# Experts' results that leave by indirect transfers, and norm factors with a token on each partition

## The reference

```python
def rmsnorm_2(x, g):
    xf = x.astype(jnp.float32)
    y = xf * lax.rsqrt(jnp.mean(xf * xf, axis=-1, keepdims=True) + EPS)
    return (y * g.astype(jnp.float32)).astype(x.dtype)

def swiglu_2(t, w_gu, w_dn):
    g, u = jnp.split(t @ w_gu, 2, axis=-1)
    return (jax.nn.silu(g) * u) @ w_dn
```

## Time and profile before

| | |
|---|---|
| three runs | 3429.14, 3432.21, 3434.34 us (median 3432.21) |
| the profiled execution | 3431.26 us, of which the span is 3429.4 |
| mean granted clock of TensorE | 0.983 |
| PE busy | 3291.8 us, 96% |
| DVE, ACT, POOL busy | 2001.3, 1767.8 and 1211.6 us |
| DMA | 555.34 MB; 531.62 read from HBM, 41.94 written |

### The profile page before, as it was taken

One profiled execution on the slowest core, in us unless ns is written; L12 is line 12 of the kernel. 1 busy time (PEld: TensorE's weight loads), 2 busy tenths in 40 slices (PEclk: granted clock), 3 DMA queues, 4 the chain that ended last, 5 costly groups with the idle time before them and its releaser, 6 DMA issues.

```text
span 3429.4 us, 48281 instructions
## 1 busy us (share of the span) xinstructions
PE 3291.8 (96%) x16320; PEld 2646.2 (77%) x16320; DVE 2001.3 (58%) x2489; ACT 1767.8 (52%) x2130; POOL 1211.6 (35%) x625
## 2 busy tenths in 40 slices
PE   8999999999999999999999999898899999999996
PEld 6888887778888788888778888687666788787783
DVE  4335674653353533641663333568766798888887
ACT  5552325455524555321645533324563788888883
POOL 3444441144444344444044444342102222222224
PEclk9999999999999999999999999999899999999998
DMA  3225321022253222533322233222003899999997
GB/s 124 98 98 168 114 95 50 26 88 96 98 169 120 86 98 93 168 118 111 117 92 97 93 96 100 79 92 84 19 14 110 337 401 412 404 408 404 398 400 303
DMA packets 128099, 555.34 MB, mean 162 GB/s; under 512 B 19344, under 2 KB 19600, under 8 KB 100112
## 3 DMA queue, kind: packets, MB, share of 16 engines
q1 hardware_dynamic: 112896, 520.59, 41.6%
q0 software_dynamic: 14976, 33.58, 2.6%
q10 hardware_dynamic: 144, 0.08, 0.0%
HBM read 531.62 MB, written 41.94 MB: 167 GB/s over the span
## 4 chain that ended last, share of the span: by engine, by line
PE 60%; issue 25%; POOL 8%; DVE 5%; ACT 1%; DMA 0%; POOLq 0%; DVEq 0%; ACTq 0%
PE ps L762 17%; PE ps L764 16%; PE ps L763 16%; POOL w_lo L1814 7%; PE ps L1232 2%; PE ps L782 1%; PE ps L922 1%; PE ps L1311 1%; PE ps L947 1%; PE ps L932 1%; PE ps L1043 1%; PE ps L1061 1%; PE ps L1022 1%; PE ps L1251 0%; PE ps L1216 0%
## 5 line engine op out<-in xcount | busy, mean ns | idle before, releaser
L1814 POOL TENSOR_TENSOR w_lo<-stage_buf,w_hi 128x1024 fp32r<-128x1024 f32 (+1 forms) x396 | 971.1, 2453 | 1505.0 <-ACT w_hi L1387 1505.0
L1387 ACT ACTIVATE w_hi<-stage_buf 128x1024 fp32r<-128x1024 f32 (+1 forms) x396 | 413.9, 1045 | 1195.1 <-PE ps L764 1142.4
L762 PE MATMUL ps<-x_hi,w_hi 128*128 128x512 f32 x1984 | 776.4, 391 | 8.9 <-POOL w_lo L1814 7.9
L763 PE MATMUL ps<-x_lo,w_hi 128*128 128x512 f32 x1984 | 775.1, 391 | 0.0
L764 PE MATMUL ps<-x_hi,w_lo 128*128 128x512 f32 x1984 | 774.9, 391 | 0.0
L762 PE MATMUL ps<-hid,w_hi 128*128 128x512 f32 x1312 | 519.0, 396 | 2.6 <-issue 1.7
L764 PE MATMUL ps<-hid,w_lo 128*128 128x512 f32 x1312 | 511.7, 390 | 0.0
L763 PE MATMUL ps<-hid,w_hi 128*128 128x512 f32 x1312 | 510.9, 389 | 0.0
L762 PEld LDWEIGHTS ps<-x_hi,w_hi 128*128 128x128 f32 x1984 | 374.3, 189 | 90.6 <-POOL w_lo L1814 10.2
L764 PEld LDWEIGHTS ps<-x_hi,w_lo 128*128 128x128 f32 x1984 | 374.2, 189 | 78.3
L763 PEld LDWEIGHTS ps<-x_lo,w_hi 128*128 128x128 f32 x1984 | 374.3, 189 | 77.6
(11 more groups left out here) (398 smaller groups left out, 4879.4 us busy)
## 6 DMA issues: line engine op xcount, KB each, us to landing
stage_buf<-in_gu SPq DMA_DIRECT2D x176, 512.0 KB, 3.2
big<-in_exp_gu SPq DMA_DIRECT2D x72, 1024.0 KB, 14.0
h_buf<-in_exp_gu SPq DMA_DIRECT2D x72, 1024.0 KB, 13.9
s_buf<-in_exp_dn SPq DMA_DIRECT2D x72, 1024.0 KB, 13.9
slot_rows<-stage_buf SPq DMA_DIRECT2D x72, 512.0 KB, 13.5
stage_buf<-in_down SPq DMA_DIRECT2D x64, 512.0 KB, 3.6
stage_buf<-in_down SPq DMA_DIRECT2D x32, 384.0 KB, 3.2
sil_buf<-in_ada SPq DMA_DIRECT2D x24, 512.0 KB, 4.1
```

The lines of the kernel that those rows point to most:

```text
L762: nc.tensor.matmul(o, a_hi, b_hi, start=start, stop=False)
L763: nc.tensor.matmul(o, a_hi, b_lo, start=False, stop=False)
L1387: nc.scalar.activation(w_hi[s][:, 0:n], stage[s][:, 0:n], ACT.Copy).then_inc(upper_done, 1)
L1814: nc.gpsimd.tensor_tensor(w_lo[s][:, 0:n], stage[s][:, 0:n], w_hi[s][:, 0:n].bitcast(F32), ALU.subtract).then_inc(parted, 1)
```

## The change

**Results.** SP no longer stores whole blocks. GpSimd writes them with an indirect transfer (`scatter`) that takes each of the 128 rows to its token and choice in `slots`, now [4, 128, 8, 1024]; rows of empty slots are out of bounds and not written. In each turn GpSimd waits for `tx` as before and now also for the evacuation of the block before (`evacuated`), converts two columns of indices, asks for the gather of block n+3, and behind it for the scatter of block n-1. Four scatters follow the loop. The 32 fetches at the end are plain transfers issued by SP. The first turn is written out on ScalarE and GpSimd, as it has nothing to scatter.

**Tables.** The token's number and the choice's go into one value, so `at_b` is made with 32 DVE operations (compare, times the value) in place of four DVE comparisons and four ScalarE scalings; `tab_f` is computed from the result with three more DVE operations; `slot_i` is gone.

**Norm factors.** For four norms (ffn1_0, norm1, first, norm2) and the four heads TensorE's sums go to one column for each 128 tokens (`token_sums`), so root and reciprocal are 128x4. TensorE then spreads the reciprocals over the partitions again (`token_rows`: four matmuls with the unit matrix), and DVE multiplies from PSUM or copies first (`spread_scale`). The table of the root is loaded earlier in two places, and each head's output is made two steps later.

```diff
-        slot_f, slot_i = small[:, 0:32], small[:, 32:64].bitcast(I32)
+        slot_f = small[:, 0:32]
...
-                    def store_rows(i, s):
-                        sp.wait_ge(bk["oev"], i * 2 + (s + 3))
-                        sp.dma_start(dr["slots"][bass.ds(i * 2 + s, 1), :, :].rearrange("a p n -> p (a n)"), o_sb[s].bitcast(I32)
-                                     ).then_inc(o_out[s], 16)
-
...
+                    def fetch(row, t, k, done):
+                        sp.dma_start(row.bitcast(I32), dr["slots"][t, :, k, :]).then_inc(done, 16)
...
+            def token_sums(bank, src, first=True, last=True):
+
+                for t in range(TT):
+                    ins = nc.tensor.matmul(ps[:, bank, t:t + 1], src[:, t * P:t * P + P], ones[:, 0:1],
+                                           start=(first and t == 0), stop=(last and t == TT - 1))
+                return ins
+
+            def token_rows(bank):
+
+                for t in range(TT):
+                    ins = nc.tensor.matmul(ps[:, bank, t * P:t * P + P], inv_tok[:, t:t + 1].to_broadcast([P, P]), eye[:, :],
+                                           start=True, stop=True)
+                return ins
...
-                    def gather(s, b, n):
-
-                        nc.gpsimd.tensor_copy(idx[:, s:s + 1], tab_f[:, b]).then_inc(bk["staged"], 1)
+                    def entry(s, b, n, c0, c1):
+
+                        nc.gpsimd.tensor_copy(idx[:, s, c0:c1], table[:, b, c0:c1]).then_inc(bk["staged"], 1)
                         pool.wait_ge(bk["staged"], n)
                         pool.sem_inc(bk["asked"], 1)
+
+                    def gather(s):
+
                         nc.gpsimd.indirect_dma_start(
                             out=xg[s], out_offset=None, in_=dr["tok"],
-                            in_offset=bass.IndirectOffsetOnAxis(ap=idx[:, s:s + 1], axis=0),
+                            in_offset=bass.IndirectOffsetOnAxis(ap=idx[:, s, 0:1], axis=0),
                             bounds_check=T - 1, oob_is_err=False).then_inc(gathered[s], 16)
 
+                    def evacuated(n):
+                        pool.wait_ge(bk["oev"], n + 2)
+                        pool.sem_inc(bk["asked"], 1)
+
+                    def scatter(s):
+
+                        nc.gpsimd.indirect_dma_start(
+                            out=dr["slots"].rearrange("t p k n -> (t p k) n"),
+                            out_offset=bass.IndirectOffsetOnAxis(ap=idx[:, s, 1:2], axis=0),
+                            in_=o_sb[s].bitcast(I32), in_offset=None,
+                            bounds_check=T * TOP_K - 1, oob_is_err=False).then_inc(o_out[s], 16)
+
...
+                    def one_block(i, s, first=False):
+                        pool.wait_ge(bk["tx"], i * 2 + (s + 2))
+                        pool.sem_inc(bk["asked"], 1)
+                        if not first:
+                            evacuated(i * 2 + s)
+                        entry(1 - s, bass.ds(i * 2 + (s + 3), 1), i * 2 + (s + 4), 0, 1 if first else 2)
+                        gather(1 - s)
+                        if not first:
+                            scatter(1 - s)
+
+                    one_block(0, 0, first=True)
+                    one_block(0, 1)
+                    with pool.Fori(1, more_n) as i:
                         for s in range(2):
-                            pool.wait_ge(bk["tx"], i * 2 + (s + 2))
-                            gather(1 - s, bass.ds(i * 2 + (s + 3), 1), i * 2 + (s + 4))
...
+                            one_block(i, s)
+                    one_block(more_n, 0)
+                    for j in range(4):
+                        evacuated(more_n * 2 + (j + 1))
+                        entry(j % 2, bass.ds(more_n * 2 + (j + 4), 1), more_n * 2 + (j + 5), 1, 2)
+                        scatter(j % 2)
...
             def hgrn_head_out(hd):
 
-                dve.wait_ge(hg["o_std"], hd + 1)
-                link(nc.vector.reciprocal(rstd[:, :], std[:, :]))
+                dve.wait_ge(hg["o_sq"], hd + 1)
                 link(nc.vector.scalar_tensor_tensor(out=mixed[:, hd, :], in0=ps[:, 4 + hd % 2, :],
-                                                    scalar=col("hg_g")[:, hd:hd + 1], in1=rstd[:, :],
+                                                    scalar=col("hg_g")[:, hd:hd + 1], in1=tiles(big[:, R_HG:R_NQ], T)[:, hd, :],
                                                     op0=ALU.mult, op1=ALU.mult))
-                nc.vector.tensor_tensor(mixed[:, hd, :], mixed[:, hd, :], tiles(big[:, R_HG:R_NQ], T)[:, hd, :],
+                dve.wait_ge(factor, FACTOR_AT[f"head{hd}"] + 2)
+                nc.vector.tensor_tensor(mixed[:, hd, :], mixed[:, hd, :], ps[:, 6 if hd < 3 else 7, :],
                                         ALU.mult).then_inc(hg["o_out"], 1)
...
                 dve.wait_ge(tab["filled"], 1)
-                nc.vector.tensor_scalar(tab_f, ps[:, 6, 0:BLOCKS], float(NO_ROW), None, ALU.add).then_inc(tab["in"], 1)
+                link(nc.vector.tensor_scalar(tab_v, ps[:, 6, 0:BLOCKS], float(2 * T * TOP_K), None, ALU.add))
+
+
+                link(nc.vector.tensor_scalar(tab_f, tab_v, 1.0 / TOP_K, 0.5 / TOP_K - 0.5, ALU.mult, ALU.add))
+                link(nc.vector.tensor_scalar(tab_f, tab_f, 12582912.0, None, ALU.add))
+                nc.vector.tensor_scalar(tab_f, tab_f, -12582912.0, None, ALU.add).then_inc(tab["in"], 1)
```

More of the change, by code:

```diff
@@ L249, in block_kernel @@
         SUM_BANK = {n: 3 if n == "first" else 2 if n in ("ffn1_1", "norm1") else 7 for n in NORMS}
+        BY_TOKEN = ("ffn1_0", "norm1", "first", "norm2")
+        FACTOR_AT = {"ffn1_0": 0, "norm1": 2, "first": 4, "head0": 7, "head1": 9, "head2": 11, "head3": 13, "norm2": 15}
+        std_tok, inv_tok = std[:, 8:8 + TT], std[:, 16:16 + TT]
         TILE_N = {n: KD * k for k, n in enumerate(TILEWISE)}
@@ L866, in token_major @@
                         last.then_inc(units_done, 1)
+                        if phase == "tok_2" and c == 0 and n == 0:
+                            spread_factor("first")
             def ada_sums(st):
@@ L1433, in raw_operand, with root_table @@
                 nc.scalar.activation(o, a, ACT.Copy, scale=g).then_inc(x_hi_ready, 1)
+            def root_table():
+                link(nc.scalar.activation(std[:, 0:1], eps[:, 0:1], ACT.Sqrt))
             def norm(name, part=True, shift=None):
-                link(nc.scalar.activation(std[:, 0:1], eps[:, 0:1], ACT.Sqrt))
+                if name not in ("norm1", "norm2"):
+                    root_table()
                 if name in SUMMED_ON_PE:
@@ L1779, in _ @@
                             raw_part(s, 1, i * 16 + 32, (bk["gu"], i * 2 + (s + 2)))
-                            evacuate(s, i)
+                            evacuate(s, i, first)
+                    two_blocks(0, first=True)
+                    with act.Fori(1, more_n + 1) as i:
+                        two_blocks(i)
                     hidden_high(0, more_n + 1)
@@ L1896, in _ @@
[L1896 to L1905, removed]
-                            if k < 2 and t % 2 == 0:
-                                pool.wait_ge(raw_parted[t // 2], more_n * 2 + (3 + k))
-                            fetch(rows[k * TT + t], t, k, row_in[k])
@@ L1909, in _ @@
-                    for i, (t, k) in enumerate(LATE):
-                        if i == 0:
-                            for s in range(2):
-                                pool.wait_ge(o_out[s], more_n * 16 + 32)
-                            pool.wait_ge(o_out[0], more_n * 16 + 48)
-                        if k == 7 and t == 0:
-                            pool.wait_ge(o_out[1], more_n * 16 + 48)
-                        pool.wait_ge(fin["row"], max(i, k == 4 and 4 * t) + 1)
-                        fetch(rows[i], t, k, row_last[t] if k == 7 else row_in[t])
+                    entry(0, slice(2, 3), 3, 0, 1)
@@ new lines, in _ @@
+                    gather(0)
+                    def one_block(i, s, first=False):
[5 more added lines that the diff above has]
+                        gather(1 - s)
+                        if not first:
+                            scatter(1 - s)
```

154 lines of the change are left out of this document (105 added, 49 removed).

## The result

The changed kernel takes 3476.43 us (median of 4 runs, 3474.53 to 3480.0) where the kernel before takes 3433.28 (median of 4, 3429.14 to 3434.91) in the same comparison: 1.0129 times as long, with a 95% interval of 1.0116 to 1.0143. It is slower by 43 us, where +37 were forecast (3469). The profiled execution has a span of 3472.7 us, so the two spans differ by 43.3 us.

A forecast was written before the change was run, and what follows sets the result against it. The loop of 72 blocks was taken as bound first by TensorE, then by the transfers. 3431.26 + 50 - 0.9 - 1.5 + 0.5 - 6.8 - 0.4 - 4 = 3468, so 3469 against the runs' median; range 3402 to 3502.

The forecast's parts named there:

- a request behind the evacuation makes 2T = 12.9 + L: Routed blocks: gather request leaves 12.9 us after its own block's turn starts, rows needed two turns after that start.
- L: Routed blocks: time from a gather's request to its landing, taken as 7.9 us, bounds 4.3 and 9.0.
- T: Routed blocks: length of one turn, 6.45 + L/2 once L exceeds 6.04 us; forecast 10.4 against 9.66 before.
- the term +50: Routed blocks: loss from late gathers, (10.4 - 9.66) x 68 = +50 us.
- the lock theory: Loop's gathers: 3 us of L is GpSimd kept from its descriptors while DVE subtracts (L2582).
- A: Rival, loop: L falls to 6 us or less as queues drain between loads; 3406 us, deciding at L = 6.0; chance 0.24.
- B: Rival, loop: L between 6.2 and 7.0, T 9.55 to 9.95; 3412 to 3439 us; chance 0.12.
- C: Rival, loop: TensorE's waits grow to 3 us and its clock falls after them; L = 10 alone gives 3540; chance 0.06.
- sums with one column save as much as the spreading costs: norm1: operands follow the reciprocal at once, so the new form gains -1.5 us (-1 to -2.3).
- The heads: Four heads: DVE is the bound; 12.6 us come off its reciprocals, TensorE gets 0.9 x 4 more; -6.8 us (-3 to -9).
- norm2 to the loop: norm2 and tables: factors sooner, 1.0 us counted for the router, 0.65 given back; -0.4 us (+1 to -1.5).
- The tail: After the loop: SP fetches not held by DVE, four stores less, earlier end of last loads; -4 us (0 to -8).

The follow-up runs named there:

- the runs with smaller loads: Changed kernel with every weight load of the loop cut to an eighth, or to half, of its columns: 3405.32 and 3411.25 us.
- gather first: Changed kernel with the gather asked for ahead of the wait for the evacuation, the scatter behind it: 3415.25 us, 0.9958 of the kernel before.
- the run with the wait alone: Kernel before, stores still by SP, with only the wait for the evacuation put ahead of each gather of the loop: 3517.0 us, 1.0252 of the kernel before.
- norm1 whole: Changed kernel with norm1's sums, root, reciprocal and table load as in the kernel before: 3468.83 us, 1.0108 of the kernel before.
- with the gather first as well: Changed kernel with both the gather ahead of the wait and norm1 as in the kernel before: 3407.53 us, 0.9932 of the kernel before.

## Why the prediction was right, and where its reasons were not

**The loop.** The step that decides, a request behind the evacuation makes 2T = 12.9 + L, stood, and the two runs that part wait and scatter show that it is the wait alone. L was taken at 7.9 and was 7.6; T at 10.4 and was 10.33; the term +50 was +45.8. That the sum comes within 8 us of the measured 3476 is in part luck: the loop's term was 4.2 us too high and norm1's 6.9 too low.

**Why L stays high: wrong.** The step that failed is "I read 3 us of L as GpSimd being kept from its descriptors by L2582". The runs showed the contrary in both directions: without the hold L is 8.4, and with it but few bytes L is 4.1. What makes the 4 us ahead of the first packet is the other transfers. The number came out because they were still at 0.94 to 0.97 of the time. That was luck: L was bounded by rows, but the reason given for its staying high was not the one at work. Two readings misled me: in the unstalled loop DVE's operation stands at the same place behind every request, so that any constant delay seems to follow it; and the fetch of the tail in the earlier trace rows was one case. Its 3353.65 is the end of a stretched request; from that request's start it took 2.7 us to the packets, not 0.6, at a DMA share of 0.89.

The Trainium skill's rule of the shared port pair ("SBUF — State Buffer", section "SBUF: two separate sides") agrees with the trace for GpSimd's CAST, 1.17 us beside DVE's subtraction and 0.18 beside a write. It doesn't carry the lock theory: for an operation with two inputs in SBUF the section names only GpSimd operations that read SBUF, and of held descriptors it tells only for DVE operations in a mode with two ports, such as an fp32 copy. The runs agree with that too: a gather's packets start in the midst of the subtraction. Another rule of the Trainium skill, that access to HBM is slower under load ("DMA: Bandwidth & Descriptors", section "Latency and other measured facts"), has the direction that the runs show, first packets after 1.6 us at a share of 0.32 and 4.0 us at 0.94; whether it is the memory's latency or the place in a queue, they don't part.

**Rivals.** A had the point at which it decides right, 6.0 us, and the runs with smaller loads reach it: 9.47 a turn. It did not come true since the bytes saved, 0.29 MB of 3.90 a block, do next to nothing for L: gather first moves the same fewer bytes, and its L is 8.2 against 8.3. B and C did not come true; C's clock did in the run with the wait alone, at 0.97.

**norm1: wrong, by 6.9 us.** The step that failed is "sums with one column save as much as the spreading costs". TensorE's rows of the sums and of the spreading, with the windows beside them (norm1, then norm2 where the same eight records come again):

```profile
2174.66 10.40 PE L780 MATMUL ps<-ones,sq_buf 128*128 128x1 f32 x48 [1.79 <-ACT sq_buf L1493]
2185.62 2.08 PE L787 MATMUL ps<-eye,std 128*128 128x128 f32 x8 [0.56 <-DVE std L2014]
...
2597.44 1.05 PE L780 MATMUL ps<-ones,acc 128*128 128x1 f32 x8
```

```profile
2174.00:2185.00 11.00, 10.34 (x48) 10.31 (x48) 2.38 (x7) 4.10 (x6) 0.93 (x1) 0.51 0.14 48
2597.00:2600.00 3.00, 3.00 (x28) 2.78 (x27) 0.35 (x2) 2.18 (x4) 1.22 (x2) 1.00 0.26 98
```

Eight records, one of the eight tiles, cost 10.40 / 6 = 1.73 us at a granted clock of 0.51, its lower level of 1.2 GHz, and 1.05 at 1.00. At the full clock the form with one column costs what the form with 512 did (1.12 for an L758 in the kernel before); PEld is busy as long as PE, which suggests that the time goes into loading the squares as weights. Ahead of the fall TensorE had done sixteen such records in 1.84 us and waited 1.79. In the kernel before the sums ran at a clock of 1.00 (2171 to 2180).

The wait of 1.79 us is the change's own. ScalarE now loads the table of the root ahead of the last six squares, where it stood behind all eight (the changed kernel, then the kernel before):

```profile
2172.35 1.28 ACT L1506 ACT_TABLE_LOAD   x1
...
2178.16 1.28 ACT L1436 ACT_TABLE_LOAD   x1
```

So the sums end 6.1 us later than before, counted from their start: 6 x 0.68 = 4.1 us by the clock (six tiles, not the eight of the run's expectation) and 1.8 by the wait. The spreading takes 2.08 us, 1.0 of them by the clock, and 3.2 are won on the reciprocal; the first matmul of in_2, counted the same way, starts some 4.3 us later, and in_2 goes on at the lower clock (0.51 from 2185 to 2195, against 0.83 before). In the five other kernels with this form the same 48 records take 10.37 to 10.40 us, so the fall is no accident of one execution. But norm1 whole puts back the form and the place of the table load at once: it shows that the two together cost 4.8 us there (5.3 with the gather first), and no run parts the form from the wait as the cause of the fall.

**The heads: right.** L2349's 13.4 us became

```profile
L2441 DVE RECIPROCAL std<-std 128x4 f32<-128x4 f32 x4 | 0.7, 166 | 0.0
```

and 5.2 us arrived behind the heads, 6.4 with out_2, of a forecast 6.8.

**norm2 to the loop: right up to the tables, then lost.** The first gather went out 1.65 us sooner (2660.04 against 2661.69), and the loop did not start sooner. The last thing ahead of it:

```profile
2659.14 8.70 PE L1285 MATMUL ps<-stage_buf,s_buf 128*128 128x512 f32 x16 [2.31 <-issue]
```

```profile
2659.00:2663.00 4.00, 3.85 (x6) 1.74 (x7) 0.00 (x0) 0.27 (x1) 2.09 (x4) 0.58 1.01 426
```

The same sixteen records took 7.11 us before, at a clock of 1.00 and behind a wait of 1.58 us; here they take 8.70, at 0.58 behind 2.31. The engine's clock fell around that wait, and the slower clock took the gain; the five other kernels with this code show the same, 8.55 to 8.72 us behind 2.31 to 2.34. The length of the wait alone isn't the rule: with norm1 whole the wait is 2.74 us and the clock stays at 1.00 there, and with the gather first as well it is 2.50 and the records take 8.62. What decides it stays open.

**The tail: right in sign.** -2.5 for -4. DVE's last wait is longer, 7.19 us in place of 6.64, but it ends 46.8 us after the last turn's start in place of 49.2, and that is the gain.

## What to carry to other kernels

An engine that issues transfers in order is a queue of promises: before a wait is put ahead of a request, count from which event the request now runs to the turn that needs it, and compare that with the landing time under full load, not with the idle one. The same two operations in the other order cost nothing here: gather, then wait and scatter, is some 59 us faster than the change (0.9958 against 1.0129). And when a transfer seems to start at the end of another engine's operation, look for turns in which that operation stands elsewhere before believing it.

## What the hardware showed that I had not expected

- The time from an indirect request to its first packet is not fixed: 1.7 us at a DMA share of 0.32, 2.1 at 0.71, 4.1 at 0.94 (medians over the loop), in the same kernel with the same GpSimd and DVE work.
- DVE's subtraction doesn't hold a gather's packets, but it stretches a request that GpSimd issues beside it: 2.64 us for the scatter's in one turn, against 1.01 on the average where DVE only writes.
- GpSimd's CAST of 128x2 takes 0.18 us or ends with DVE's subtraction (1.17 us), for a tensor_tensor and a scalar_tensor_tensor alike; beside a DVE write of the same size it takes 0.18.
- 128x1 sums, with the data as weights, cost TensorE as much as 128x512 sums by ones (1.05 against 1.12 us), and in six kernels that do them behind a wait of 1.79 to 1.80 us the clock fell to 0.51.
- With TensorE busy all 100 us at 387 GB/s (gather first), the DMA share reads 1.00, and the kernel before moved 407 GB/s at 1.01: a share of 1.00 alone doesn't say that the transfers are the bound.
